# A fused two-block kernel: high products first in each quarter, other points for sigmoids, rotations and weight copies, and residual additions by DVE

## The reference

```python
def hybrid_layer(h, ...):                      # once
    z = rmsnorm(h, g_pre) @ w_in
    aq, ak, av, ag, hq, hf_f, hf_b, hv, hg = split(z)
    ...                                        # dilated attention, two recurrent scans
    y = concatenate([y_att, y_hg]) @ w_out
    h = h + rmsnorm(y, g_post)
    gate = sigmoid(h @ w_pg)
    return h + rmsnorm(gate * (p_l @ w_pp), g_ple)

for l in range(2):                             # second block
    proj = rms_norm(x, pre_norm_g[l]) @ w_in[l]
    (rq, rk, rv, rg, dq, dk, dv, dg, lx, lg) = split(proj)
    ret_out  = rms_norm(retention(rope(rq), rope(rk), rv)) * silu(rg)     # 6 heads of 128
    diff_out = rms_norm(diff_attention(rope(dq), rope(dk), dv, lam), g) * (1 - lam_init) * silu(dg)
    #          4 heads, each softmax(q0 k0) - lam * softmax(q1 k1), causal, in 4 blocks of 128 queries
    lru_out  = rg_lru(lx, ...) * silu(lg)                                 # 768 wide, causal scan
    x = x + rms_norm(concatenate([ret_out, diff_out, lru_out]) @ w_out[l], post_norm_g[l])
```

## Time and profile before

| | |
|---|---|
| median of three runs | 3059.6 us (3057.93 to 3060.82) |
| profiled execution: its own time | 3061.06 us |
| profiled execution: span | 3059.1 us |
| granted PE clock, mean over the span | 0.991 |
| busy: PE, DVE, POOL, ACT | 2979.6, 1621.2, 1384.5, 1304.7 us |
| PE instructions (matmuls) | 17338 |
| POOL, low parts L340 | 844 of 1351 ns in the mean |
| ACT, high parts L861 | 832 of 629 ns |
| HBM read and written | 293.01 and 18.35 MB, 102 GB/s over the span |

### The profile page before, as it was taken

How to read it: one execution, slowest core, us unless ns; L and a number is a source line. 1 busy time by engine, 2 the same in 40 slices (tenths; PEclk the granted TensorE clock), 3 DMA queues, 4 the chain that set the end, 5 groups by cost and what they waited for, 6 DMA issues and landing times.

```text
span 3059.1 us, 48606 instructions
## 1 busy us (share of the span) xinstructions
PE 2979.6 (97%) x17338; PEld 2409.3 (79%) x17338; DVE 1621.2 (53%) x2383; ACT 1304.7 (43%) x2552; POOL 1384.5 (45%) x1050
## 2 busy tenths in 40 slices
PE   8999999999999999999999999999999999999998
PEld 6888888777776887877878877778878788777786
DVE  5377666655657215643556565551445565655412
ACT  6545444454547333444333333443443333334432
POOL 4444444433333456554444433344744444333444
PEclk9999999999999999999999999999999999999999
DMA  6222222222222334324322222233343222222333
GB/s 242 103 88 105 80 82 82 82 72 82 82 82 70 138 123 138 110 97 148 117 90 87 90 83 73 79 138 103 117 149 117 90 87 90 83 69 81 140 101 105
DMA packets 79009, 313.30 MB, mean 102 GB/s; under 512 B 7440, under 2 KB 11920, under 8 KB 51472
## 3 DMA queue, kind: packets, MB, share of 16 engines
q1 hardware_dynamic: 54832, 266.62, 25.7%
q10 hardware_dynamic: 24032, 44.76, 4.2%
HBM read 293.01 MB, written 18.35 MB: 102 GB/s over the span
## 4 chain that ended last, share of the span: by engine, by line
issue 46%; POOL 27%; PE 22%; DVE 2%; ACT 1%; POOLq 1%; DMA 0%; DVEq 0%; ACTq 0%; SPq 0%
POOL w_low L340 26%; PE z L418 13%; PE scores L418 1%; DVE u_low L1943 1%; PE z L483 1%; PE scores L436 1%; PE scores L437 1%; PE v_bank L483 1%; POOLq L339 1%; PE scores L440 1%; POOL pass_weights L363 1%; PE scores L443 0%; DMA w_raw<-in_wt 0%; PE turned L436 0%; PE turned L437 0%
## 5 line engine op out<-in xcount | busy, mean ns | idle before, releaser
L340 POOL TENSOR_TENSOR w_low<-w_raw,w_high 128x512 fp32r<-128x512 f32 x844 | 1135.7, 1351 | 1541.7 <-ACT w_high L861 1519.2
L418 PE MATMUL z<-u_high,w_high 128*128 128x512 f32 x3216 | 1277.4, 397 | 15.5 <-POOL w_low L340 14.8
L418 PE MATMUL z<-u_high,w_low 128*128 128x512 f32 x3216 | 1257.3, 391 | 0.0
L418 PE MATMUL z<-u_low,w_high 128*128 128x512 f32 x3216 | 1256.1, 391 | 0.0
L861 ACT ACTIVATE w_high<-w_raw 128x512 fp32r<-128x512 f32 x832 | 519.8, 629 | 1121.0 <-PE z L418 1080.8
L418 PEld LDWEIGHTS z<-u_high,w_high 128*128 128x128 f32 x3216 | 606.3, 189 | 165.6 <-issue 37.5
L418 PEld LDWEIGHTS z<-u_high,w_low 128*128 128x128 f32 x3216 | 605.9, 188 | 129.5
L418 PEld LDWEIGHTS z<-u_low,w_high 128*128 128x128 f32 x3216 | 606.8, 189 | 120.5
L1878 DVE TENSOR_TENSOR work<-work 128x512 f32<-128x512 f32 x78 | 92.6, 1187 | 277.8 <-ACT work L1150 264.7
L1502 DVE TENSOR_TENSOR work<-z,work 128x512 f32<-128x512 f32 x110 | 76.1, 692 | 189.3 <-PE z L418 150.5
L363 POOL TENSOR_TENSOR pass_weights<-w_raw,pass_weights 128x512 fp32r<-128x512 f32 x96 | 133.9, 1412 | 46.6 <-ACT pass_weights L1063 46.2
(11 more groups left out here) (342 smaller groups left out, 3771.7 us busy)
## 6 DMA issues: line engine op xcount, KB each, us to landing
w_raw<-in_wt SPq DMA_DIRECT2D x213, 1024.0 KB, 4.9
w_raw<-in_wt SPq DMA_DIRECT2D x144, 256.0 KB, 2.9
out_hT<-work ACTq DMA_DIRECT2D x10, 1024.0 KB, 6.8
work<-out_hT ACTq DMA_DIRECT2D x8, 1024.0 KB, 10.4
work<-in_xT SPq DMA_DIRECT2D x4, 1024.0 KB, 16.8
e_scratch<-work ACTq DMA_DIRECT2D x1, 4096.0 KB, 16.8
work<-in_xT ACTq DMA_DIRECT2D x4, 1024.0 KB, 11.0
mixed<-e_scratch ACTq DMA_DIRECT2D x4, 1024.0 KB, 11.2
```

The lines of the kernel that those rows point to most:

```text
L340: pool.tensor_tensor(WL[:, 4 * q:4 * q + 4, :], RAW[:, t.odd, 512 * q:512 * q + 512].rearrange("p (k c) -> p k c", k=4), WH[:, 4 * q:4 * q ...
L418: mm = pe.matmul(bank[:], w[:, k, :], u[:, k, :], start=(k == 0 and n == 0), stop=(k == KT - 1 and n == 2))
```

## The change

The change moves work; it adds and removes no matmul. In the diff's order:

- **The output's last stores**: only the constants of two waits change their unit.
- **POOL**: `add_pair` is gone. POOL no longer adds pairs of rows in the four regions; only the two wide additions at the end of the program stay.
- **`quarter`** (PE): it waits for the high part (`h_ready`), issues the eight matmuls with WH, waits for the low part (`l_ready`), and issues the four with WL.
- **`norm_points`** (PE): in the gate region the token row and the turn back go from behind pieces 9 and 11 of a pass to behind pieces 6 and 7.
- **Steps** (ACT, DVE): in the last step of a difference attention the sigmoids and the gate products of the three lru gates go behind the work of slots 7, 11 and 15. The gate of the step before goes from ahead of slot 0 to slot 3.
- **`THIRD_PASS`** (ACT): the ten weight copies of pass 2 go to four places ahead of the second half's norm work and six behind it.
- **`residual_half`** (DVE): each pair of rows is scaled and added before the next pair; all rows count on `h_new`.
- **`pg_bounded`** (DVE): the clamps of the gate region's second half stand ahead of the seventh low part of the first half.
- **Difference attention** (DVE): `ends` goes from (4, 9) to (6, 10), so the rotations stand behind the softmax of block 1 and of block 2.

```diff
@@ -363,23 +363,11 @@
-            def add_pair(n, h, i, m):
-
-                pool.wait_ge(sem("tile_scaled"), 4 * n + i + 1)
-                pool.tensor_tensor(W[:, H + m:H + m + 2, half(h)], W[:, H + m:H + m + 2, half(h)], MIX[:, m:m + 2, half(h)],
-                                   ALU.add).then_inc(sem("h_pool"), 2)
-
-            def low_region(r, first):
+            def low_region(r):
...
                     low_piece(t, s)
-                    for h, at in ((0, (20, 21, 22, 23)), (1, (30, 31, 32, 33))) if r == 1 else ((0, (19, 20, 21, 22)), (1, (29, 30, 31, 32))):
-                        if s in at and h == 0 or s in at and t + 2 * PASS < NT:
-                            add_pair(2 * r + h, h, at.index(s), first + 2 * at.index(s))
-                if r == len(REGIONS) - 1:
-                    for i in range(1, 4):
-                        add_pair(2 * r, 0, i, first + 2 * i)
@@ -389,11 +377,11 @@
                 low_tiles(done, REGIONS[r])
-                low_region(r, 4 if t is None else 0)
+                low_region(r)
                 done = REGIONS[r] + 2 * PASS
             for m, count in ((0, 1), (3, 2)):
-                pool.wait_ge(sem("tile_scaled"), 4 * LAST_HALF + count)
+                pool.wait_ge(sem("tile_scaled"), count)
                 pool.tensor_tensor(W[:, H + m:H + m + 3, half(1)], W[:, H + m:H + m + 3, half(1)], MIX[:, m:m + 3, half(1)],
@@ -410,13 +398,15 @@
                         pe.wait_ge(sem("z_free"), t.times(1, 1 - T_HGG - behind))
-                pe.wait_ge(sem("l_ready"), t.times(4, q + 1))
+                pe.wait_ge(sem("h_ready"), t.times(4, q + 1))
                 for k in range(4 * q, 4 * q + 4):
...
                         pe.wait_ge(sem("u_ready"), gen * 16 + k + 1)
-                    for n, (w, u) in enumerate(((WH, UH), (WH, UL), (WL, UH))):
-                        mm = pe.matmul(bank[:], w[:, k, :], u[:, k, :], start=(k == 0 and n == 0),
-                                       stop=(k == KT - 1 and n == 2))
+                    pe.matmul(bank[:], WH[:, k, :], UH[:, k, :], start=(k == 0), stop=False)
+                    pe.matmul(bank[:], WH[:, k, :], UL[:, k, :], start=False, stop=False)
+                pe.wait_ge(sem("l_ready"), t.times(4, q + 1))
+                for k in range(4 * q, 4 * q + 4):
+                    mm = pe.matmul(bank[:], WL[:, k, :], UH[:, k, :], start=False, stop=(k == KT - 1))
                 mm.then_inc(sem("w_free"), 1)
@@ -780,8 +770,8 @@
                 if pg:
-                    return {9: lambda: root_row(n),
-                            11: lambda: turn_back(n, (sem("pg_prod"), 14 + 2 * h), h, (0, 12), BACK_PG[h])}
+                    return {6: lambda: root_row(n),
+                            7: lambda: turn_back(n, (sem("pg_prod"), 14 + 2 * h), h, (0, 12), BACK_PG[h])}
                 return {3: lambda: root_row(n),
@@ -804,9 +794,9 @@
                 first = l == 0
-                one_pass(l + 1, 2, base - 3, l + 1, ORDERS[l + 1], updated=2 * 8 + 4 if first else None,
+                one_pass(l + 1, 2, base - 3, l + 1, ORDERS[l + 1], updated=2 * KT + 12 if first else None,
                          between=norm_points(l + 1, 1, first))
-                one_pass(l + 1, 3, base, l + 1, ORDERS[l + 1], updated=3 * 8 + 4 if first else None)
+                one_pass(l + 1, 3, base, l + 1, ORDERS[l + 1], updated=3 * KT + 12 if first else None)
                 for m in range(LRU_TILES):
@@ -1045,8 +1035,8 @@
                         gate_sigmoid(gate)
-                    if gates is not None and q == 3:
-                        gate_sigmoid(gates + s)
+                    if gates is not None and p in (7, 11, 15):
+                        gate_sigmoid(gates + p // 4 - 1)
@@ -1072,7 +1062,7 @@
             SECOND_PASS = dict(zip((1, 2, 3, 4, 6, 7, 9, 10, 12, 13), range(16, 26)))
-            THIRD_PASS = dict(zip((0, 2, 3, 5, 6, 8, 9, 11, 12, 14), range(26, 36)))
+            THIRD_PASS = dict(zip((-4, -3, -2, -1, 1, 2, 3, 4, 5, 6), range(26, 36)))
             LAST_PASS = dict(enumerate(range(16, 20)))
@@ -1109,7 +1099,7 @@
                 m = ORDERS[g][n]
-                act.wait_ge(sem("h_new" if n >= 8 else "h_pool"), (2 * g + h) * 8 + n % 8 + k)
+                act.wait_ge(sem("h_new"), (2 * g + h) * KT + n + k)
                 if g == 0:
@@ -1423,7 +1413,7 @@
                 step(Tile(T_L2 + R_DIF + 4, (PER_LAYER, l)), gate=l * 16 + 24, work="dif", j=l * DIF_HEADS, quarters=THREE,
-                     between={0: lambda: gate_sigmoid(l * 16 + 23)})
+                     between={3: lambda: gate_sigmoid(l * 16 + 23)})
                 for i in range(2, DIF_HEADS):
@@ -1800,14 +1789,14 @@
                             rstd_mul(t.plus(3), row(VT))
-                    if lru is not None and THREE.get(p, (0, 0))[1] == 3:
-                        s = THREE[p][0]
-                        lru_gate(t.plus(s), lru + s, s + 1)
                     if work is not None:
...
                         between[p]()
+                    if lru is not None and p in (7, 11, 15):
+                        s = p // 4 - 1
+                        lru_gate(t.plus(s), lru + s, s + 1)
                     if hg is not None and p in (4, 8, 12):
@@ -1914,18 +1903,15 @@
-            def residual_half(n, h, loaded, others, own, turned, banks, gain):
+            def residual_half(n, h, loaded, tiles, turned, banks, gain):
...
                 v.wait_ge(sem("h_loaded"), loaded)
-                for m in others:
-                    scale_tiles(m, 2, h).then_inc(sem("tile_scaled"), 1)
-                for m in own:
+                for m in tiles:
                     scale_tiles(m, 2, h)
-                v.drain()
-                for m in own:
+                    v.drain()
                     add_tiles(m, 2, h)
@@ -1944,9 +1930,11 @@
-            def low_halves(g, h):
+            def low_halves(g, h, between={}):
                 for n in range(0, KT, 4 if g == 0 else 1):
+                    if n in between:
+                        between[n]()
                     low_half(g, h, n, 4 if g == 0 else 1)
@@ -2119,12 +2107,15 @@
-            def pg_last(h):
+            def pg_bounded(h):
...
                                     ).then_inc(sem("z_free"), 2 if r == 15 else 1)
+
+            def pg_last(h):
+
                 for r in (12 + 2 * h, 13 + 2 * h):
@@ -2138,9 +2129,11 @@
             for h in range(2):
+                if h == 0:
+                    pg_bounded(0)
                 pg_last(h)
-                residual_half(2 + h, h, 64, range(4, 12, 2), (), (0, 1, 2, 3, 12, 13, 14, 15), BACK_PG[h], PR1[:, G_PLE:G_PLE + 16])
-                low_halves(1, h)
+                residual_half(2 + h, h, 64, range(4, 12, 2), (0, 1, 2, 3, 12, 13, 14, 15), BACK_PG[h], PR1[:, G_PLE:G_PLE + 16])
+                low_halves(1, h, {6: lambda: pg_bounded(1)} if h == 0 else {})
@@ -2167,11 +2160,11 @@
                          ret=l * RET_HEADS + h, gate=(gl + h, h), work="ret", j=l * RET_HEADS + h - 1, m=h - 1)
-                dif = dict(rot=(CTD, STD, 32), scales=scd, take="dqt_ready", ends=(4, 9), gate_tile_at=2)
+                dif = dict(rot=(CTD, STD, 32), scales=scd, take="dqt_ready", ends=(6, 10), gate_tile_at=2)
                 step(Tile(T_L2 + R_DIF, (PER_LAYER, l)), gate=(gl + 6, 6), work="ret", j=l * RET_HEADS + RET_HEADS - 1, m=5,
                      **{**dif, "ends": (3, 7)})
-                lru_gate(Tile(T_L2 + R_DIF + 3, (PER_LAYER, l)), gl + 7, 0)
-                step(Tile(T_L2 + R_DIF + 4, (PER_LAYER, l)), gate=(gl + 8, 7), work="dif", j=l * DIF_HEADS, m=6, **dif)
+                step(Tile(T_L2 + R_DIF + 4, (PER_LAYER, l)), gate=(gl + 8, 7), work="dif", j=l * DIF_HEADS, m=6,
+                     between={3: lambda: lru_gate(Tile(T_L2 + R_DIF + 3, (PER_LAYER, l)), gl + 7, 0)}, **dif)
                 for i in range(2, DIF_HEADS):
@@ -2195,10 +2188,10 @@
                 n, gain = 2 * l + 4, PR2[:, l, G2_POST:G2_POST + 16]
-                residual_half(n, 0, l * 64 + 128, range(0, 8, 2), (8, 10), (12, 13, 14, 15), BACK, gain)
+                residual_half(n, 0, l * 64 + 128, range(0, 12, 2), (12, 13, 14, 15), BACK, gain)
                 if l + 1 < LAYERS:
                     low_halves(l + 2, 0)
-                    residual_half(n + 1, 1, l * 64 + 128, range(0, 8, 2), (8, 10), (12, 13, 14, 15), BACK, gain)
+                    residual_half(n + 1, 1, l * 64 + 128, range(0, 12, 2), (12, 13, 14, 15), BACK, gain)
                     low_halves(l + 2, 1)
```

More of the change, by code:

```diff
@@ L322, in _ @@
                     sp.wait_ge(sem(f"w_part{q}_{o}"), 16 * sum((b - a + 1 - o) // 2 for a, b in PASS_TILES))
-            n = LAST_HALF * 8
+            n = LAST_HALF * KT
             for c, a, b in ((4, 12, 16), (10, 6, 12)):
@@ L1473, in _ @@
                 passing(l + 2, LAST_PASS if last else SECOND_PASS, norm_work(l + 2, 0, None if last else l + 2))
-            act.wait_ge(sem("h_new"), LAST_HALF * 8)
```

(6 more changed lines are left out.)

## The result

The changed kernel takes 3033.36 us (median, 3031.75 to 3035.2) beside 3059.06 us for the one before: a ratio of 0.9916 (95% interval 0.9898 to 0.9933), 25.7 us faster. The direction was right; the prediction, 3045 us with a range from 3037, was short by 11 us.

What follows compares the result with a forecast made beforehand. PE was taken as the bound, busy 2979.6 of 3059.1 us, so only idle and low-clock time could go. Terms -1.2, -2.4, -3.2, -0.9, -7.2 sum to -14.9 us: median 3045 us, range 3037 to 3057.

Steps and rivals of the forecast that it cites:

- the gate region: Passes at 1358 to 1383 us: 7.1 us of waits and 2.7 of clock go, token-scale waits come; -3.2 us.
- The attention: Difference attention in both layers: -8.8 us of waits and clock, +5.2 for new waits per layer; -7.2 us in all.
- the term for the new waits: PE waits before o_bank products, second and third attention step: 1.6 or 2.65 us, taken as +2.1 plus 0.5 clock each.
- the first region: Passes at 1180 to 1188 us: PE's 2.4 us of waits go, with DVE's low halves having time to spare; -2.4 us.
- the layer region: First layer's passes at 2221 to 2225 us: 1.4 us of waits go, +0.5 at the token scale; -0.9 us.
- The additions and THIRD_PASS: DVE adding row pairs and pass 2's weight copies moved earlier: together remove 11.0 us of PE's pass waits.
- The clock: PE's granted clock drops after long waits: 2.7 us lost in the gate region, 1.7 behind a 2.5 us wait.
- high products first: In each quarter, eight matmuls cover POOL's low part; removes one true low-part wait, -1.2 us, semaphore cost taken as 0.
- the two big stalls: One per layer behind the last retention head: PE waits for DVE's gate-bank read, not POOL's low part; 14.8 us stays.
- the chain to the o_bank wait: Attention slots 6 to 8: the moved rotation delays DVE's dif_done, so PE waits about 2 us before its values.
- the length of a pair of DVE operations: DVE's scaling plus addition of a row pair in the regions: 1.3 to 2.4 us, taken as 1.85.
- the port: Slower rival: DVE's two-input operations and POOL's low parts exclude each other throughout; 22 us more, 3067 us; chance 0.08.

## Why the prediction was wrong

**The attention was the step that failed.** The mechanism was foreseen; the term for the new waits was too dear, 2.6 us each where they cost 1.5. Forecast: -8.8 for what goes and +5.2 for what comes, a layer. What went measured 9.6 by matching places (1.0 for each of three softmax waits that the profile gives as 0.84; 2.7, 1.7 and 2.2 in the last step), and the two new waits cost 1.53 each with no low clock behind them, not 2.6: 3.1 a layer. So the net is 6.5 instead of 3.6. The two ends of that bound were 1.6 and 2.65 us, and I took the mean of the two with a clock loss on top, though I had myself noted that waits of 2.0 us and less mostly show no such loss. The low end was right because DVE's addition began ahead of POOL's operation there, by 0.06 us: no row of the kernel before could settle which of the two would be first. Over both layers that is 5.9 of the 12.9 us by which the two profiled executions (27.8 apart) go beyond the sum.

**The regions** gave more than foreseen, 5.0 for 3.2 in the gate region and 3.6 for 2.4 in the first. The new waits were sized right (1.4 and 3.0 for 1.7 and 2.9, and 1.1 in the layer region for 0.5; clock 1.4 for 2.0). What was too small is what went: several waits cost PE more than their label. The softmax waits of 0.84 cost 1.0 each, and in the first region four waits, 2.4 us by label, were 3.6 by matching places, 0.3 more for each. It is no fixed surplus: the new waits of 1.53 moved the matching instruction by 1.56. The 2.8 us that went out of "busy" are of this size; no run isolates them.

**The additions and THIRD_PASS** were priced as one edit with one cause. Here the mechanism was wrong, not only a size: either one takes nearly all waits for weights in the passes away, so they do not add, and the early copies also stand ahead of the squares on which the token scale hangs. The additions alone gain 13.7 us, of which 12.0 by matching places in the three regions, where the changed kernel with both gained 9.8; the copies gain nothing alone and cost 6.9 beside the additions. The prediction's working held the price, 5 us from the second half's products to its token scale with the copies between, but never put it beside the same sum without them. Measured, it is 6.2 us with the early copies and 4.8 without.

**The clock** was counted as -2.1 net and gave 7.0 in the profiled pair. In the foreseen places 5.9 went (6.1 foreseen) and 1.4 came (4.0 foreseen, of which 2.0 behind the o_bank waits, where none came). The other 2.5 lie where the change moves nothing, 1.5 of them in the windows from 648 to 656: there the same wait costs clock in one execution and not in another. Five executions with the gates undone lie between 3044.5 and 3052.4 us at mean clocks of 0.994 to 0.991.

**Right:** high products first (-1.2), the two big stalls, their cause and that they stay; the chain to the o_bank wait; the length of a pair of DVE operations (1.7 for 1.85, a middle value taken between two bounds), and that the port does not decide. The Trainium skill, "SBUF — State Buffer", section "Who interferes with whom", says that a DVE instruction with two SBUF inputs contends with a GpSimd instruction that reads SBUF, and that issue order decides who blocks. The prediction read from it that every addition would take its long form; the traces agree with the order instead. Before, POOL began 0.1 us ahead of the long addition of the earlier trace rows and kept its usual time:

```profile
1896.67 1.30 POOL L340 TENSOR_TENSOR w_low<-w_raw,w_high 128x512 fp32r<-128x512 f32 x1 [1.42 <-ACT w_high L861]
```

In the rows of the new wait DVE began first, kept its 0.69 us, and POOL took 1.75. Over the whole trace of the changed kernel, the additions of L1898 and L1527 began inside a running POOL operation 59 times: each ended 0.55 to 0.61 us behind the end of that operation, so it took between 0.69 and 1.75 us by how much of POOL's was left. The 8 that began ahead of one took 0.69. That is where the median of 1.02 comes from.

Left open: why a wait of 1.5 us is followed by a low clock in one execution and not in the next, and the 1.1 us behind the last token row.

## What to carry to other kernels

When two edits remove the same wait, price each alone and both together, and look at what each puts ahead of the next chain: here the second edit gained nothing alone and cost 6.9 us beside the first. When a piece of work is moved to a later slot, try the slot behind that one too: the order of three pieces around one signal (softmax, output, rotation) was worth 6.8 us. And when the named releaser had long been done, move the event that ended just before the restart: reading one bank four slots earlier was worth 15 us.

## What was not expected of the hardware

Some waits cost PE more than their label (1.0 for 0.84, 3.6 for four of 2.4 in all), others did not (1.56 for 1.53). A low clock (0.67 in one window) followed a wait of 1.54 us in one of eighteen profiled executions and in none of the others. Of a DVE addition and a POOL subtraction that meet, the later one is stretched: 0.69 and 1.75 us when DVE began 0.06 us earlier, 1.75 and 1.30 when it began 0.1 us later, and in 59 of 59 cases a DVE addition that began second ended 0.55 to 0.61 us behind POOL's operation.
